# First expert step of a mixture-of-experts layer: token rows by zero-one products on TensorE in place of an indirect DMA

## Chip, cores and metric

One core of a Trainium2 chip. The metric is the device time of one execution in microseconds (us), lower is better. A moment such as 1291.30 is counted in us from the start of the profiled execution.

## What is computed

The program runs two transformer stacks on 256 tokens of width 1024. The change touches only the end of each of the second stack's two layers (`DEPTH = 2`, 272 tokens with the 16 meta tokens), its mixture of experts:

```
grp_prob = softmax(t @ w_grp + b_grp); g_prob, g_sel = top_k(grp_prob, 1)
in_grp = the 8 expert logits of the chosen group; e_prob, e_sel = top_k(softmax(in_grp), 2)
combine = one_hot(8 * g_sel + e_sel, 32) * gate, summed over the two
hid = silu(t @ w1[e]) * (t @ w3[e])
y = sum over e of (hid * combine) @ w2[e]
h = layer_norm(ALPHA * h + y)
```

There are 32 experts; `w1` and `w3` are 1024 x 256 each, `w2` is 256 x 1024, all float32. Every token goes to two of them.

## The kernel before

Tokens live mostly as `hT` (features on partitions). After the first layer norm of a layer they are also turned into rows, `h_tok` (tokens on partitions, three blocks of 128, 128 and 16, `TOK`), which lies in `h_area`. ScalarE writes those rows (six copies, each counted on the semaphore `htok_ready`), and SyncE stores them to HBM as `h_rows` (L944).

**Steps.** The experts are taken in 8 groups of 4. A step `s` serves one group: four experts side by side with 32 token slots each, 128 slots in all. A group in which an expert has more than 32 tokens takes further steps. The profiled input has 24 steps, 12 in each layer. VectorE computes the router's outcome: `comb` (gates), `rank` (the place of a token in its expert), and from them for a step a zero-one matrix `sel` (token x slot, 3 blocks; `select`, L2897 to 2905, counted on `sel_ready`). `sel` and `slot_cols` are single buffers. TensorE multiplies `sel` with `slot_cols` (`slots`, L1692 to 1697, PSUM bank `UP`) and gets for each slot its gate and its token number; VectorE copies these out (`slots_out`, L2907 to 2913). GpSimd turns the token number into an index and fetches the 128 rows from `h_rows` in HBM with an indirect DMA (`fetch`, L2242 to 2248, semaphore `rows_in`) into `x_rows`, which is the first block of `h_tok`. TensorE transposes the rows (`turn_rows`, L1699 to 1704, eight transposes into the banks `ROWS`), ScalarE copies them into `x_g` (L2189 to 2194), and the step proper starts (`expert_step`, L1716): 64 instructions of the up part (L1724), then the rows of the next step are turned, then the down part (L1746) and the sum into the output banks (L1757, L1759).

**First step of a layer.** `slots(start)`, then `hold_clock(..., 10)`: ten products of constants (L1177) whose result is overwritten, then the wait for the fetched rows, `turn_rows` twice, and `slots(start + 1)`. VectorE meanwhile computes how many steps each group needs (L2917 to 2950, `steps_ready`) and the selection of the second step (`select_at(start + 1)`).

**Expert weights.** A group's weights are 12 pieces of 1 MB, written (group, piece) below, each loaded by SyncE in one DMA (`expert_load`, all at L929) into one of 22 places. 22 pieces are loaded ahead of the loop, each as soon as its place is free. From (1, 10) on, a load waits in SyncE's program order for the step that gives its place free: pieces 0 to 7 of a group use the place of an earlier group's `w1`, `w3` and wait for the up part of that group's last step (`loop_full[UP]`, L961). Pieces (1, 4) and (1, 5) lie in `h_area` over the second and third blocks of `h_tok`; (1, 4) waits for the store to `h_rows` (`rows_out`).

Of the kernel before, what the change touches and what calls it, by code (L numbers as in the profile page):

```python
# [16 lines left out]
P = 128  # L17
# [99 lines left out]
def build(nc, A, out):  # L117

    ctx = ExitStack()
    with ctx:  # L120
# [750 lines left out]
        def _(sp):  # L871
# [37 lines left out]
            for slot, parts, last, *more in chunk_order:  # L909
# [10 lines left out]
                if slot == "experts":  # L920
# [24 lines left out]
                    sp.wait_ge(comb_ready, l + 1)  # L945
                    expert_load(1, 3)
                    expert_load(1, 9)
                    sp.wait_ge(rows_out, 48 * (l + 1))
                    expert_load(1, 4)
                    b, u = tiles[("rk", l)]  # L950
                    sp.wait_ge(full[b], u)
                    expert_load(1, 0)
                    for g in range(1, 8):
                        for m in range(10 if g == 1 else 0, 12):
                            g0, m0 = divmod(12 * g + m - XS, 12)
                            if m0 == 0:
                                if g0 == 0:
                                    sp.wait_ge(steps_ready, l + 1)

                                last = sp.value_load(steps[0:1, l, g0 + 10:g0 + 11], min_val=0, max_val=1000)  # L960
                                sp.wait_ge(loop_full[UP], up_use(last, l, 1))  # L961
                            elif m0 == 8:
                                end = sp.value_load(steps[0:1, l, g0 + 1:g0 + 2], min_val=1, max_val=1000)
                                sp.wait_ge(loop_full[ROWS[1]], row_use(end, l, 0))
                            expert_load(g, m)
# [21 lines left out]
        def _(pe):  # L987
# [186 lines left out]
            def hold_clock(b, count):  # L1174

                for _ in range(count):
                    nc.tensor.matmul(ps[:, b, 0:S1], ones[:, :], held, start=True, stop=True)  # L1177
# [197 lines left out]
            for l in range(DEPTH):  # L1375
# [311 lines left out]
                def begin_l(b, before):  # L1687

                    pe.wait_ge(loop_free[b], before + 1)
                    return b  # L1690
# [8 lines left out]
                def turn_rows(a, before):  # L1699
# [3 lines left out]
                        last = nc.tensor.transpose(ps[:, b, k * P:(k + 1) * P], x_rows[:, (4 * a + k) * P:(4 * a + k + 1) * P], ident)  # L1703
                    last.then_inc(loop_full[b], 1)

                pe.wait_ge(sel_ready, start + (2 * l + 1))
                slots(start, up_use(start, l, -2))
                hold_clock(begin_l(ROWS[0], row_use(start, l, -1)), 10)
                pe.wait_ge(rows_in, start * 16 + 16 * (l + 1))
                for a in range(2):  # L1710
                    turn_rows(a, row_use(start, l, -1))
                pe.wait_ge(sel_ready, start + (2 * l + 2))
                slots(start + 1, up_use(start, l, -1))
                pe.wait_ge(steps_ready, l + 1)
# [1 line left out]
                def expert_step(s, g):  # L1716
# [10 lines left out]
                                                    start=(k == 0), stop=(k == KT - 1))  # L1727
                    last.then_inc(loop_full[b], 1)

                    pe.wait_ge(rows_in, s * 16 + 16 * (l + 2))  # L1730
                    turn_rows(0, row_use(s, l, 0))
                    pe.wait_ge(ehid_ready, s + 1)
                    b = begin_l(UP, up_use(s, l, 1))
# [482 lines left out]
        def _(pool):  # L2216
# [7 lines left out]
            for l in range(DEPTH):  # L2224
                if l == 0:
                    pool.wait_ge(const2_in[0], 16 * 10)
                for lv in range(7):
                    for n in range(3):
                        if lv >= LV[n]:
                            continue  # L2230
                        L = TOK[n][1]
                        if lv == 0:
                            pool.wait_ge(lt_ready, 3 * l + n + 1)
                        else:
                            b, u = tiles[("X", l, lv - 1, n)]
                            pool.wait_ge(full[b], u)
                            if lv == 1:
                                pool.wait_ge(t_ready, t_at[l][(0, n)])
                        nc.gpsimd.tensor_tensor(heads(As[:, n, :])[0:L, :, 0:L], heads(LT[:, n, :])[0:L, :, 0:L],  # L2239
                                                levels[0:L, lv, 0:L].unsqueeze(1).broadcast_to([L, DH, L]), ALU.mult).then_inc(as_ready, 1)  # L2240

                def fetch(s):  # L2242

                    pool.wait_ge(slots_ready, s + (2 * l + 1))
                    nc.gpsimd.tensor_copy(row_of[:, :], slot_token[:, bass.ds(s, 1)])  # L2245
                    nc.gpsimd.drain()
                    nc.gpsimd.indirect_dma_start(x_rows, None, h_rows, bass.IndirectOffsetOnAxis(ap=row_of[:, :], axis=0))\
                        .then_inc(rows_in, 16)

                start = 0 if l == 0 else pool.value_load(steps[0:1, 0, 8:9], min_val=1, max_val=MAX_STEPS // 2)  # L2250
                pool.wait_ge(rows_out, 48 * (l + 1))
                fetch(start)
                pool.wait_ge(loop_full[ROWS[1]], row_use(start, l, 0))
                fetch(start + 1)
                pool.wait_ge(steps_ready, l + 1)
                last = pool.value_load(steps[0:1, l, 17:18], min_val=1, max_val=MAX_STEPS - 4)
                with nc.gpsimd.Fori(start, last) as s:
                    pool.wait_ge(loop_full[ROWS[1]], row_use(s, l, 1))
                    fetch(s + 2)
# [3 lines left out]
        def _(dve):  # L2263
# [303 lines left out]
            for l in range(DEPTH):  # L2567
# [386 lines left out]
                def select_at(s):  # L2954

                    g = dve.value_load(step_group[0:1, bass.ds(s, 1)], min_val=0, max_val=7)
                    select(g, pass_at[:, bass.ds(s, 1)])

                select_at(start + 1)
                slots_out(start + 1, up_use(start, l, 0))  # L2960
                stop = dve.value_load(steps[0:1, l, 8:9], min_val=1, max_val=MAX_STEPS - 3)
# [52 lines left out]
```

## Time and profile before

| | |
|---|---|
| time, median of 3 runs | 2179.34 us (2172.04 to 2183.63) |
| span of the profiled execution | 2178.0 us |
| the profiled execution's own time | given by its span alone; it lies 1.3 us under the median |
| TensorE busy | 92% of the span |
| VectorE, ScalarE, GpSimd busy | 43%, 34%, 32% |
| expert steps | 12 in layer 0 (from 1305.34), 12 in layer 1 (from 1905.94) |

A page of the profile gives busy time, granted TensorE clock ("PEclk") and DMA load by slices of the span, then the groups of instructions with what each waited for. The timeline of an engine lists its instructions in order: start, length, engine, line, operation, tiles, and in brackets how long the engine had been idle and what ended that. PE is TensorE, PEld its weight loads, DVE VectorE, ACT ScalarE, POOL GpSimd, SP SyncE; a letter q behind an engine is its sequencer. A float32 product shows as two records in the timeline, a transpose as one. The granted clock is 1.00 at 2.4 GHz and 0.50 at 1.2 GHz.

### The profile page before, as it was taken

The numbers are of one execution on the slowest core, as the hardware profiler recorded it, in microseconds if no ns is written. First come the engines' busy times: TensorE is split into PE (matmuls) and PEld (weight loads), VectorE is DVE, ScalarE is ACT, GpSimd is POOL, SyncE is SP. The second block draws the span as 40 slices with busy tenths as digits, with TensorE's granted clock in tenths as the row PEclk, the third lists the DMA queues.
The fourth block names the chain that finished last, engine by engine and source line by source line (L and its number), as shares of the span: only waits on it lengthen the run. The fifth ranks groups of instructions, "written<-read, shape, count | busy, mean of one in ns | idle before, by whom it ended". The sixth has DMA issues, their size and how long they took to land.

```text
span 2178.0 us, 36546 instructions
## 1 busy us (share of the span) xinstructions
PE 1999.3 (92%) x14251; PEld 1596.2 (73%) x14255; DVE 939.0 (43%) x1852; ACT 744.1 (34%) x1189; POOL 698.8 (32%) x558
## 2 busy tenths in 40 slices
PE   7989999999999999999999988759999999889966
PEld 6779899998889999987868763324578787634424
DVE  6562436615543456416754351111347643512212
ACT  5554543345555443413322222112223222222212
POOL 6557648885757558810003000000000030000000
PEclk9999999999999999999998989879999999999988
DMA  7335335553345345553310368999233203688693
GB/s 232 100 113 167 123 117 194 172 179 121 130 144 166 116 156 192 176 176 109 125 58 1 136 262 363 420 421 364 106 141 117 97 2 136 262 350 357 280 420 157
DMA packets 196269, 405.95 MB, mean 186 GB/s; under 512 B 18515, under 2 KB 143846, under 8 KB 171286
## 3 DMA queue, kind: packets, MB, share of 16 engines
q1 hardware_dynamic: 192374, 390.20, 48.8%
q0 software_dynamic: 3744, 13.63, 1.6%
q8 instruction: 107, 1.75, 0.3%
q14 instruction: 44, 0.36, 0.1%
HBM read 400.53 MB, written 3.28 MB: 185 GB/s over the span
## 4 chain that ended last, share of the span: by engine, by line
PE 71%; DVE 8%; DMA 7%; ACT 5%; SPq 3%; issue 2%; DVEq 2%; POOL 2%; ACTq 1%; POOLq 0%
PE ps L1017 9%; PE ps L1018 9%; PE ps L1356 9%; PE ps L1019 9%; PE ps L1724 7%; DMA weight_ring<-in_w 3%; PE ps L1746 3%; PE ps L1621 3%; SPq L929 3%; POOL weight_ring L2223 2%; DVEq L2266 1%; DMA last_pair<-in_w 1%; DMA spare<-in_w 1%; PE ps L1091 1%; PE ps L1560 1%
## 5 line engine op out<-in xcount | busy, mean ns | idle before, releaser
L2223 POOL TENSOR_TENSOR weight_ring<-weight_ring 128x512 fp32r<-128x512 f32 (+1 forms) x466 | 630.0, 1387 | 308.6 <-ACT weight_ring L1821 291.0
L1017 PE MATMUL ps<-weight_ring 128*128 128x256 f32 x1824 | 528.8, 290 | 12.4 <-DVE acts L2340 5.0
L1019 PE MATMUL ps<-weight_ring 128*128 128x256 f32 x1568 | 440.0, 281 | 0.0
L1018 PE MATMUL ps<-acts,weight_ring 128*128 128x256 f32 x1472 | 415.2, 282 | 0.0
L1017 PEld LDWEIGHTS ps<-weight_ring 128*128 128x128 f32 x1824 | 345.3, 189 | 25.5 <-issue 24.7
L1019 PEld LDWEIGHTS ps<-weight_ring 128*128 128x128 f32 x1568 | 298.4, 190 | 0.0
L1018 PEld LDWEIGHTS ps<-acts,weight_ring 128*128 128x128 f32 x1472 | 279.0, 190 | 1.9 <-issue 1.4
L1821 ACT ACTIVATE weight_ring<-weight_ring 128x2048 fp32r<-128x2048 f32 x128 | 238.7, 1883 | 92.0 <-PE ps L1019 82.8
L1356 PE MATMUL ps<-acts,weight_ring 128*128 128x272 f32 x896 | 212.8, 396 | 2.7 <-ACTq L2170 1.4
L2245 POOL CAST row_of<-slot_token 128x1 uint32 (+1 forms) x26 | 4.8, 186 | 625.1 <-DVE slot_token L2910 625.1
L1356 PEld LDWEIGHTS ps<-acts,weight_ring 128*128 128x128 f32 x896 | 170.3, 191 | 40.9 <-issue 2.4
L2239 POOL TENSOR_TENSOR acts<-work,tables 128x512 f32<-128x512 f32 (+1 forms) x36 | 38.4, 1090 | 465.2 <-DVE work L2710 398.7
L1724 PE MATMUL ps<-weight_ring,x_g 128*32 128x512 f32 x816 | 137.0, 654 | 32.3 <-DMA last_pair<-in_w 24.2
L1724 PE MATMUL ps<-acts,x_g 128*32 128x512 f32 x320 | 100.1, 628 | 26.6 <-DMA spare<-in_w 13.4
L2295 DVE TENSOR_TENSOR weight_ring<-weight_ring 128x512 fp32r<-128x512 f32 (+1 forms) x62 | 85.9, 1418 | 64.9 <-ACT weight_ring L1821 64.9
L2970 DVE SCALAR_TENSOR_TENSOR score<-score,slot_gate,ps 128x256 f32<-128x256 f32 x24 | 11.5, 481 | 237.5 <-ACT score L2199 237.5
L2199 ACT ACTIVATE score<-ps 128x256 f32<-128x256 f32 x24 | 9.2, 385 | 283.3 <-PE ps L1724 283.3
L1018 PE MATMUL ps<-qkv,weight_ring 128*128 128x256 f32 x352 | 99.6, 283 | 0.0
L1724 PEld LDWEIGHTS ps<-weight_ring,x_g 128*32 128x32 f32 x816 | 35.0, 119 | 87.8 <-issue 87.0
L1724 PE MATMUL ps<-spare,x_g 128*32 128x512 f32 x176 | 85.9, 646 | 0.0
L2978 DVE TENSOR_TENSOR z_gate<-ps,e_out 128x512 fp32r<-128x512 f32 x48 | 33.2, 692 | 118.2 <-ACT e_out L2205 118.2
L1724 PE MATMUL ps<-h_area,x_g 128*32 128x512 f32 x144 | 70.0, 643 | 14.1 <-DMA weight_ring<-in_w 14.1
(479 smaller groups left out, 3753.8 us busy)
## 6 DMA issues: line engine op xcount, KB each, us to landing
weight_ring<-in_w SPq DMA_DIRECT2D x112, 1024.0 KB, 22.8
weight_ring<-in_w_gate_up SPq DMA_DIRECT2D x44, 1024.0 KB, 5.0
weight_ring<-in_w_in SPq DMA_DIRECT2D x16, 2048.0 KB, 9.2
acts<-in_w SPq DMA_DIRECT2D x32, 1024.0 KB, 24.6
weight_ring<-in_x_wkv SPq DMA_DIRECT2D x16, 1024.0 KB, 5.3
weight_ring<-in_w_down SPq DMA_DIRECT2D x16, 1024.0 KB, 4.9
spare<-in_w SPq DMA_DIRECT2D x16, 1024.0 KB, 26.7
h_area<-in_w SPq DMA_DIRECT2D x16, 1024.0 KB, 23.5
```

The costliest lines, as they stand in the source:

```text
L929: sp.dma_start(expert_weights(g, m), src).then_inc(expert_in[pair_of(g, m)], 16)
L1017: nc.tensor.matmul(o, wh, xh, start=start, stop=False)
L1018: nc.tensor.matmul(o, wh, xr, start=False, stop=False)
L1019: return nc.tensor.matmul(o, wr, xh, start=False, stop=stop)
L1356: last = nc.tensor.matmul(ps[:, b, 0:S2], ring[:, slot, at + k * step:at + k * step + P], hT[:, k, :], start=(k == 0), stop=(k == KT - 1))
L1621: last = nc.tensor.matmul(ps[:, b, 0:S2], ring[:, s, at:at + P], oT[:, k, :], start=(k == 4), stop=(k == 3))
L1724: last = nc.tensor.matmul(ps[32 * j:32 * j + 32, b, :].rearrange("p (a n) -> p a n", a=2), x_g[:, k, 32 * j:32 * j + 32], expert_weights(g ...
L1746: last = nc.tensor.matmul(ps[32 * j:32 * j + 32, b, :], e_hidT[:, f, 32 * j:32 * j + 32], expert_weights(g, 8 + j)[:, at:at + 512], start= ...
L1821: nc.scalar.activation(r12(high[:, n % HIGH, 0:w]), raw[:, n % RAW, 0:w], ACT.Copy).then_inc(high_ready, 1)
L2223: nc.gpsimd.tensor_tensor(r12(w), w, r12(high[:, n % HIGH, part]).bitcast(F32), ALU.subtract).then_inc(rest_ready, 1)
L2239: nc.gpsimd.tensor_tensor(heads(As[:, n, :])[0:L, :, 0:L], heads(LT[:, n, :])[0:L, :, 0:L], levels[0:L, lv, 0:L].unsqueeze(1).broadcast_to ...
L2295: nc.vector.tensor_tensor(r12(w), w, r12(high[:, n % HIGH, 3 * k * 64:4 * k * 64]).bitcast(F32), ALU.subtract).then_inc(rest_ready4, 1)
```

## The change

The rows of the first step of each layer are no longer fetched. TensorE multiplies the token rows on chip with the selection: for each of 8 blocks of 128 features, three float32 products (one for each block of tokens, accumulated in PSUM), 24 in all, whose result is what the transposes gave before. They stand where the ten products of constants and the eight transposes stood. VectorE now makes the second step's selection only when these products are done, since they read `sel`; GpSimd's first fetch is that of the second step. The load of (1, 4), which overwrites rows that the products read, waits for them and goes behind (1, 0).

```
--- before
+++ after
@@ SyncE, behind the store of h_rows
                     expert_load(1, 3)
                     expert_load(1, 9)
-                    sp.wait_ge(rows_out, 48 * (l + 1))
-                    expert_load(1, 4)
                     b, u = tiles[("rk", l)]
                     sp.wait_ge(full[b], u)
                     expert_load(1, 0)
+                    start = 0 if l == 0 else sp.value_load(steps[0:1, 0, 8:9], min_val=1, max_val=MAX_STEPS // 2)
+                    sp.wait_ge(rows_out, 48 * (l + 1))
+                    sp.wait_ge(loop_full[ROWS[1]], row_use(start, l, 0))
+                    expert_load(1, 4)
@@ TensorE, first step
+                def gather_rows(a, before):
+
+                    b = begin_l(ROWS[a], before)
+                    for k in range(4):
+                        at = (4 * a + k) * P
+                        for n, (t0, L) in enumerate(TOK):
+                            last = nc.tensor.matmul(ps[:, b, k * P:(k + 1) * P], h_tok[0:L, n, at:at + P], sel[0:L, n, :],
+                                                    start=(n == 0), stop=(n == 2))
+                    last.then_inc(loop_full[b], 1)
+
+                pe.wait_ge(htok_ready, 6 * (l + 1))
                 pe.wait_ge(sel_ready, start + (2 * l + 1))
                 slots(start, up_use(start, l, -2))
-                hold_clock(begin_l(ROWS[0], row_use(start, l, -1)), 10)
-                pe.wait_ge(rows_in, start * 16 + 16 * (l + 1))
                 for a in range(2):
-                    turn_rows(a, row_use(start, l, -1))
+                    gather_rows(a, row_use(start, l, -1))
                 pe.wait_ge(sel_ready, start + (2 * l + 2))
                 slots(start + 1, up_use(start, l, -1))
...
-                    pe.wait_ge(rows_in, s * 16 + 16 * (l + 2))
+                    pe.wait_ge(rows_in, s * 16 + 16)
@@ GpSimd
                 pool.wait_ge(rows_out, 48 * (l + 1))
-                fetch(start)
                 pool.wait_ge(loop_full[ROWS[1]], row_use(start, l, 0))
                 fetch(start + 1)
@@ VectorE
+                dve.wait_ge(loop_full[ROWS[1]], row_use(start, l, 0))
                 select_at(start + 1)
```

TensorE in layer 0, from the first selection's products to the first up part, before and then changed (ISA and TENSOR_LOAD are its sequencer's; the loads read which steps the first group has):

```order
L1696 MATMUL ps<-slot_cols,sel 128x5 x3
L1177 MATMUL ps<-tables,ones 128x256 x10
L1703 MATMUL ps<-tables,h_area 128x128 x8
L1696 MATMUL ps<-slot_cols,sel 128x5 x3
L1770 TENSOR_LOAD steps
L1770 ISA x2
L1771 TENSOR_LOAD steps
```

```order
L1698 MATMUL ps<-slot_cols,sel 128x5 x3
L1714 MATMUL ps<-sel,h_area 128x128 x24
L1698 MATMUL ps<-slot_cols,sel 128x5 x3
L1781 TENSOR_LOAD steps
L1781 ISA x2
L1782 TENSOR_LOAD steps
```

Ten products of constants and eight transposes went, 24 products came; the sequencer's loads still stand behind the second selection's products.

VectorE at the same place, between the end of the step tables and the copy of the second step's token numbers, before and then changed:

```order
L2949 TENSOR_SCALAR pass_at<-pass_at 128x53
L2956 TENSOR_LOAD step_group [waits steps_ready]
L2956 ISA x2
L2899 ISA
L2899 COPY slot_cols<-comb 128x3x4
```

```order
L2959 TENSOR_SCALAR pass_at<-pass_at 128x53
L2966 TENSOR_LOAD step_group [waits loop_full2,steps_ready]
L2966 ISA x2
L2909 ISA
L2909 COPY slot_cols<-comb 128x3x4
```

The sequencer's load and all behind it now wait for `loop_full2`, the end of TensorE's new products.

SyncE behind the store of the rows, before and then changed (`acts`, `spare`, `h_area` and `last_pair` are the places of (1, 3), (1, 9), (1, 4) and (1, 0)):

```order
L944 DMA h_rows<-h_area 16x1024
L929 DMA acts<-in_w_2 128x2048 [waits comb_ready]
L929 DMA spare<-in_w_2 128x2048
L929 DMA h_area<-in_w_2 128x2048 [waits rows_out]
L929 DMA last_pair<-in_w_2 128x2048 [waits psum_full0]
L960 TENSOR_LOAD steps [waits steps_ready]
```

```order
L944 DMA h_rows<-h_area 16x1024
L929 DMA acts<-in_w_2 128x2048 [waits comb_ready]
L929 DMA spare<-in_w_2 128x2048
L929 DMA last_pair<-in_w_2 128x2048 [waits psum_full0]
L929 DMA h_area<-in_w_2 128x2048 [waits loop_full2,rows_out]
L962 TENSOR_LOAD steps [waits steps_ready]
```

(1, 4) went behind (1, 0) and behind TensorE's new products; nothing else on this queue moved.

## Rows read from the trace of the kernel before

**Rows 1.** The page: the span, and the DMA engines' busy share in 40 slices.

```profile
span 2178.0 us, 36546 instructions
...
DMA  7335335553345345553310368999233203688693
```

**Rows 2.** The chain of waits, layer 0: start, length, what.

```profile
1289.62 0.24 issue
...
1292.77 8.95 DMA h_area<-h_rows,row_of
```

**Rows 3.** TensorE's timeline, layer 0: start, length, instruction, idle before it.

```profile
1291.30 6.08 PE L1177 MATMUL ps<-tables,ones 128*128 128x256 f32 x20
1301.77 1.97 PE L1703 MATMUL ps<-tables,h_area 128*128 128x128 f32 x8 [4.38 <-DMA h_area<-h_rows,row_of]
1303.53 1.37 PE L1696 MATMUL ps<-slot_cols,sel 128*128 128x5 f32 x6
1305.34 8.38 PE L1724 MATMUL ps<-weight_ring,x_g 128*32 128x512 f32 x64 [0.44 <-DVEq L2912]
```

**Rows 4.** TensorE's timeline, layer 1.

```profile
1892.81 7.39 PE L1177 MATMUL ps<-tables,ones 128*128 128x256 f32 x20
1903.67 1.09 PE L1703 MATMUL ps<-tables,h_area 128*128 128x128 f32 x8 [3.47 <-DMA h_area<-h_rows,row_of]
1904.60 0.82 PE L1696 MATMUL ps<-slot_cols,sel 128*128 128x5 f32 x6
1905.94 8.45 PE L1724 MATMUL ps<-weight_ring,x_g 128*32 128x512 f32 x64 [0.52 <-DVEq L2912]
```

**Rows 5.** SyncE's timeline, layer 0: the loads of expert weights.

```profile
1289.54 0.33 SPq L929 DMA_DIRECT2D h_area<-in_w  x1
...
1313.79 0.33 SPq L929 DMA_DIRECT2D weight_ring<-in_w  x1
```

**Rows 6.** Busy time by stretch: engines, then granted clock, DMA share, GB/s.

```profile
1301.50:1313.80 12.30, 11.60 (x79) 5.34 (x80) 1.76 (x8) 2.49 (x4) 1.13 (x2) 0.73 0.13 44
1314.50:1344.40 29.90, 24.77 (x205) 12.96 (x206) 7.01 (x22) 8.34 (x13) 2.27 (x4) 1.00 1.00 406
```

**Rows 7.** GpSimd's fetches: issue of the second, landings of layers 0 and 1.

```profile
1306.26 0.95 POOL L2247 DMA_INDIRECT h_area<-h_rows,row_of  x1 [0.84 <-issue]
...
DMA to landing us min/median/max: 4.4/6.7/8.9
...
DMA to landing us min/median/max: 9.3/9.3/9.3
```

**Rows 8.** TensorE's timeline, float32 products of this shape elsewhere.

```profile
1166.45 1.06 PE L1570 MATMUL ps<-weight_ring,yT 128*128 128x128 f32 x8
1167.34 1.06 PE L1568 MATMUL ps<-yT,weight_ring 128*128 128x128 f32 x8
```

**Rows 9.** Busy time and granted clock by stretch, as rows 6.

```profile
1291.30:1294.38 3.08, 3.08 (x8) 2.52 (x8) 2.55 (x10) 0.00 (x0) 1.45 (x2) 0.50 1.00 423
...
1301.60:1308.02 6.42, 5.82 (x30) 3.77 (x34) 1.40 (x7) 2.48 (x3) 1.13 (x2) 0.50 0.01 4
...
1345.80:1349.00 3.20, 3.20 (x20) 0.92 (x16) 0.00 (x0) 0.00 (x0) 0.00 (x0) 0.50 1.02 419
...
1892.81:1898.54 5.73, 5.73 (x15) 4.56 (x15) 3.89 (x15) 0.00 (x0) 1.41 (x2) 0.50 1.01 420
...
1905.68:1908.39 2.71, 2.45 (x12) 0.61 (x16) 1.02 (x7) 1.28 (x1) 1.14 (x2) 0.50 0.00 0
```

**Rows 10.** VectorE's timeline, layer 0: the second step's selection.

```profile
1295.77 0.19 DVE L2949 TENSOR_SCALAR pass_at<-pass_at 128x53 f32<-128x53 f32 x1
1297.14 0.17 DVE L2899 COPY slot_cols<-comb 128x12 f32 x1 [1.18 <-issue]
1297.27 0.88 DVE L2901 SCALAR_TENSOR_TENSOR sel<-tables,pass_at,rank 128x128 f32<-128x128 f32 x3
```

**Rows 11.** TensorE's sequencer, layer 1: its load of the first group's steps.

```profile
L1770 PEldq TENSOR_LOAD <-steps x1: 305/305/305, 1903.9 to 1903.9; - x1
```

## The prediction

> **What bounds the kernel now.** I read the page first: over a span of 2178.0 us the DMA engines are nearly full in two stretches, slices 24 to 28 and again towards the end [rows 1], which are the expert loops of the two layers. Next the chain of waits around the entry of the first loop: from 1292.77 it is one piece of 8.95 us, the indirect fetch of the first step's rows [rows 2]. TensorE's timeline shows what that means: the ten products of constants end at 1297.38, TensorE idles 4.38 us for the fetch, turns the rows, multiplies the second selection and starts the first step at 1305.34 [rows 3]. Layer 1 has the same shape: 3.47 us idle, first step at 1905.94 [rows 4]. So the entry of the loop is bounded by the fetch, twice in the program, and 4.38 + 3.47 = 7.9 us is all the idle time there is to win directly.
>
> Does an earlier start reach the end? SyncE's next expert load is issued at 1313.79, as soon as the up part ends (1305.34 + 8.38 = 1313.72) [rows 3, 5]. Before it the DMA engines are nearly empty (share 0.13), behind it full (1.00) for at least 30 us [rows 6]. The loads behind it are released by steps. An earlier first step therefore moves the whole loop, its DMA-bound stretches too, and I count a gain at the first step at its full size.
>
> **What goes.** The fetch: 8.95 us in layer 0, 9.3 in layer 1, 4.4 for the second fetch of layer 0 [rows 2, 7]. The ten products of constants, 6.08 and 7.39 us, and the eight transposes, 1.97 and 1.09 us [rows 3, 4].
>
> **What comes on the path, step by step.**
> (a) The products. 24 float32 products are 48 records. Float32 products of this shape at full clock follow each other 1167.34 - 1166.45 = 0.89 us per 8 records, 0.111 us each [rows 8]. At half clock I take twice that, 0.223; the eight transposes of layer 0, 1303.53 - 1301.77 = 1.76 us, were at 0.22 each with a granted clock of 0.50 [rows 3, 9]. The products begin where those of constants began. In layer 0 the clock there is 0.50 until 1294.38: 3.08 us, 14 records; the other 34 take 3.8 us, end at 1298.2. In layer 1 it is 0.50 for 5.73 us after 1892.81: 26 records; the other 22 take 2.5 us, end at 1901.0 [rows 4, 9]. I assume that the new products raise the clock at the same moment as the old ones, since both keep TensorE busy without a gap.
> (b) A new wait. VectorE's selection of the second step was made while the fetch ran, done by 1298.15 [rows 10]; now its sequencer waits for (a). From the end of the tables, 1295.96, to its first copy it took 1.18 us, most of it the sequencer's load of the step's group, which now stands behind the wait: 1.1 us. The selection itself: 1298.15 - 1297.14 = 1.0. From its drain to TensorE's products 0.24 us, say 0.3 [rows 2, 10]. Sum 2.4 us, all on the path. Behind VectorE's wait stand only the second step's token numbers, then the loop.
> (c) The second selection's products, then the start of the step: 0.82 + 0.52 = 1.34 us at full clock [rows 4]. But TensorE's sequencer reads the group's steps behind them; before, it did so ahead, during the transposes: from 1903.9 to the step's start at 1905.94 are 2.0 us [rows 4, 11]. Now it can't begin before the selection is ready. Bounds 1.3 and 2.0; I take 2.0, since that row is the same sequence of instructions.
> So a first step starts 2.4 + 2.0 = 4.4 us after its products end. Layer 0: 1302.6 against 1305.34, 2.7 us won. Layer 1: 1905.4 against 1905.94, 0.5 us won.
> (d) The clock in the first step. Before, a stretch at 0.50 reached 2.7 us into the up part in both layers (1305.34 to 1308.02; 1905.68 to 1908.39) [rows 9]. Now TensorE idles about 2.4 us in (b), then does light work. A similar pause elsewhere was followed by 3.20 us at 0.50 (1345.80 to 1349.00) inside an up part [rows 9], so I expect about 3 us, 0.2 us worse in each layer.
> Sum: 2.7 + 0.5 - 0.4 = 2.8, about 3 us.
>
> **What is covered.** ScalarE's copies into `x_g` follow the products and are done during (b). The load of (1, 4) was issued at 1289.54 [rows 5]; it now goes at about 1298.3, 1 MB at 406 GB/s, 2.6 us, into a time in which DMA is nearly empty [rows 6], and its group's weights are wanted only behind the first step. Nothing waits behind it on SyncE's queue but the load at 1313.79. The second fetch, issued at 1306.26, landed 4.4 us later [rows 7], 3 us before it was wanted at 1313.72. It moves with the step and meets empty DMA engines again. If that cover went, each us would cost one. GpSimd does nothing else there.
>
> A rule that speaks against the change: by the Trainium skill (DMA: Bandwidth & Descriptors, Anatomy of one DMA) a GpSimd DMA takes about 2.0 us plus bytes / 436e3, for these 512 KB 3.2 us as an estimate. By that the rows would be in at 1296.0 and 1897.6, before the products of constants end; the old first steps would start 3.57 and 2.27 us behind that end, at 1301.0 and 1902.5, and the change would lose 1.6 + 2.9, about 5 us, to some 2184. The trace disagrees, 8.95 and 9.3 us behind queued weight loads [rows 2, 7]; only the fetch that met empty engines, 4.4 us, is near the rule.
>
> **The rivals.**
> *The clock is kind* (13%). Products wholly at full clock take 48 x 0.111 = 5.3 us, end 1296.6 and 1898.1, steps start at 1301.0 and 1902.5: 4.3 and 3.4 us won, and 1.3 us more per layer if no slow stretch (2.7 us at half) falls into the step. 10.3 us, 2169. For it: the slow stretch differs by layer, 3.08 against 5.73 us [rows 9]. Against: both layers were slow at this point.
> *The clock is unkind, and the new chain is the longer one* (17%, the side of slower). Products wholly at 0.50: 48 x 0.223 = 10.7 us, end 1302.0 and 1903.5, steps at 1306.4 and 1907.9, 1.1 and 2.0 us lost, 2182. It decides when more than about 38 (layer 0) or 30 (layer 1) of the 48 records run at 0.50. If the up part were at 0.50 throughout as well, another 5.7 us each (5.70 us were at full clock): 2194, 4% of the 17. For it: layer 1 has already 26 slow records, and 5-column products and pauses surround them. Against: unbroken work did bring the clock back in both layers.
> *The gain is swallowed by the weight loads* (10%), 2179. For it: the loop is DMA-bound behind the first step. Against: its first load is released by that step, with DMA at 0.13 before it [rows 6].
> That the change doesn't do what it says I leave out: the order of instructions shows 24 products for the fetch.
>
> The Trainium skill (TensorE: Matmul & The Clock Gate, What you observe and What's actually happening) says that the half rate is the default, that activity lifts it, and that the point of the switch varies from run to run. Rows 9 agree: 3.08 and 5.73 us for the same code.
>
> **How the numbers follow.** The forecast has 60%: 2179.3 - 3 = 2176.3; the span would be 2175. Runs before scattered by 11.6 us, a median of a few by perhaps 4 us either way. The range takes the kind rival at 2169 with a little scatter and the unkind one at 2182 with some: 2168 to 2184. A measurement of this kernel can tell about 0.5%, 11 us, from no change. Faster by more: half of the kind rival and 2 of the forecast's 60, 0.09. Slower by more: 0.05 from the unkind rival's far end and scatter. Else 0.86.
>
> **What would show it.** Right: no idle time before TensorE's rows; 48 records of `sel`, `h_area` in 6 to 9 us; then about 2.4 us idle until VectorE's selection; first steps 1 to 3 us earlier, counted from the first selection's products; (1, 4) issued behind the products; the load behind the up part earlier by the same. Wrong: products much longer than 9 us, an idle TensorE before the second step's rows or before group 1's weights, or loops that end at the old distance although they begin earlier. The forecast fails most simply if the clock's phase at the two entries is another one.

## The result, and the profile after the change

| | before | after |
|---|---|---|
| time, median | 2179.2 us (2172.0 to 2183.6, 4 runs) | 2192.4 us (2188.9 to 2194.7, 4 runs) |
| ratio, 95% interval | | 1.0058 [1.0041, 1.0074] |
| profiled execution: time, span | span 2178.0 | 2188.93, span 2187.1 |
| first selection's products to the first up part, layers 0 and 1 | 15.47, 14.58 us | 20.75, 20.59 us |

The change costs 13.2 us. The forecast was 2176.3 in a range of 2168 to 2184, with 5% on slower by over 0.5%. It was wrong in sign and the range missed the time by 8 us.

(Two corrections to the sections on the kernel before. Piece (1, 4) alone covers the second and third blocks of `h_tok`; (1, 5) lies behind it. And a span is 1.8 to 1.9 us shorter than the time of the same execution in every run listed, so the profiled execution of the kernel before took about 2179.8 us, close to the median and not 1.3 us under it.)

The page after, which answers to [rows 1]:

```profile
span 2187.1 us, 36622 instructions
...
DMA  7335335553444355553310369998334103688693
```

The two stretches of full DMA are where they were. The entries are counted from the first selection's products, and the first up parts to the transposes behind them. In the kernel before these lines, which no group of rows has, stand for both layers:

```profile
1289.87 1.50 PE L1696 MATMUL ps<-slot_cols,sel 128*128 128x5 f32 x6 [0.73 <-DVEq L2905]
1313.65 0.66 PE L1703 MATMUL ps<-tables,h_area 128*128 128x128 f32 x4
1891.36 1.52 PE L1696 MATMUL ps<-slot_cols,sel 128*128 128x5 f32 x6 [1.02 <-DVEq L2905]
1914.32 0.66 PE L1703 MATMUL ps<-tables,h_area 128*128 128x128 f32 x4
```

The place of the change is shown by TensorE's timeline, layer 0, which answers to [rows 3] (L1698 are the selection's products, L1714 the new ones, L1735 the up part, L1705 the next step's transposes):

```profile
1285.72 1.50 PE L1698 MATMUL ps<-slot_cols,sel 128*128 128x5 f32 x6 [0.36 <-DVEq L2915]
1287.15 15.06 PE L1714 MATMUL ps<-sel,h_area 128*128 128x128 f32 x48
1304.42 1.53 PE L1698 MATMUL ps<-slot_cols,sel 128*128 128x5 f32 x6 [2.21 <-DVEq L2915]
1306.47 8.90 PE L1735 MATMUL ps<-weight_ring,x_g 128*32 128x512 f32 x64 [0.52 <-DVEq L2922]
1315.30 0.66 PE L1705 MATMUL ps<-tables,h_area 128*128 128x128 f32 x4
```

The same in layer 1, which answers to [rows 4]:

```profile
1893.51 1.53 PE L1698 MATMUL ps<-slot_cols,sel 128*128 128x5 f32 x6 [1.06 <-DVEq L2915]
1894.96 15.06 PE L1714 MATMUL ps<-sel,h_area 128*128 128x128 f32 x48
1912.06 1.53 PE L1698 MATMUL ps<-slot_cols,sel 128*128 128x5 f32 x6 [2.04 <-DVEq L2915]
1914.10 8.87 PE L1735 MATMUL ps<-weight_ring,x_g 128*32 128x512 f32 x64 [0.52 <-DVEq L2922]
```

Read it against steps (a) to (c). No idle time stands ahead of the new products, but they take 15.06 us in both layers, 0.314 us a record, where (a) had 6.9 and 8.2 us in all. Behind them come the 2.21 and 2.04 us of VectorE's wait, the second selection and the up part. The stretches, as [rows 9]:

```profile
1285.70:1302.21 16.51, 16.49 (x54) 12.81 (x54) 4.64 (x19) 0.60 (x1) 0.00 (x0) 0.50 0.42 172
1302.21:1306.40 4.19, 1.53 (x6) 1.43 (x6) 1.30 (x7) 1.88 (x2) 0.08 (x1) 0.50 0.73 246
1306.40:1310.12 3.72, 3.65 (x20) 1.00 (x24) 1.46 (x6) 0.00 (x0) 1.23 (x2) 0.50 0.21 76
1893.50:1910.02 16.52, 16.51 (x54) 12.82 (x54) 4.81 (x20) 0.60 (x1) 0.00 (x0) 0.50 0.36 152
```

The granted clock is 0.50 over all of them. TensorE was busy for 16.49 of 16.51 us in the first stretch, and for 16.51 of 16.52 in layer 1, and its clock did not rise; it rose only at about 1310.12, 3.7 us into the up part. The weight loads of the products in layer 0, by form (busy, mean ns, and idle time before them with its cause):

```profile
L1714 PEld LDWEIGHTS ps<-sel,h_area 128*128 128x128 f32 x32 | 7.4, 322 | 1.6 <-issue 1.6
L1714 PEld LDWEIGHTS ps<-sel,h_area 16*128 16x128 f32 x16 | 4.0, 308 | 1.8 <-issue 1.8
```

Between the loads lie 1.6 + 1.8 us put down to "issue". 48 records at half clock are 10.7 us by the prediction, so 4.4 us of the 15.06 are not the clock's, and this column holds 3.4 of them.

The other engines did as forecast. VectorE, layer 0, as [rows 10]: its selection of the second step starts after 11.51 us without work, behind the wait for the products:

```profile
1303.34 0.17 DVE L2909 COPY slot_cols<-comb 128x12 f32 x1 [11.51 <-issue]
```

SyncE, as [rows 5]: (1, 4) goes as soon as the products end, and the first load of the loop 1315.44 - 1315.30 = 0.1 us after the up part:

```profile
1302.31 0.33 SPq L929 DMA_DIRECT2D h_area<-in_w  x1
1315.44 2.58 SPq L929 DMA_DIRECT2D weight_ring<-in_w  x5
```

GpSimd, as [rows 7]: the fetch of the second step's rows and its landing, 5.5 us, during the up part:

```profile
1307.38 1.13 POOL L2258 DMA_INDIRECT h_area<-h_rows,row_of  x1 [0.88 <-issue]
...
DMA to landing us min/median/max: 5.5/5.5/5.5
```

**Where the 13.2 us are.** I cut both profiled executions at the first selection's products, at the first up part and at the transposes behind it. The entries grew by 5.28 and 6.01 us, the first up parts (to their transposes) by 0.52 and 0.43: 12.2 us. The stretch between the layers grew by 0.50 and the rest behind layer 1's by 0.51: 13.3 us. The spans differ by 9.1 only, because this execution reached the first selection 4.15 us earlier (1285.72 against 1289.87), in code that the change doesn't touch. That 13.3 is also the difference of the medians is in part luck: after's profiled execution is the fastest of its four, 3.5 us under their median.

### The profile page after: what moved, and what is told of

Its sections match the earlier page's. It is cut to its first block, busy times and chain, and to the rows that moved or that the text cites. A ratio compares the mean times of both kernels' runs of the same rounds, so it can differ in the third digit from the quotient of the medians.

```text
span 2187.1 us, 36622 instructions
## 1 busy us (share of the span) xinstructions
PE 2014.3 (92%) x14291; PEld 1605.0 (73%) x14295; DVE 938.7 (43%) x1852; ACT 744.1 (34%) x1189; POOL 695.1 (32%) x554
## 4 chain that ended last, share of the span: by engine, by line
PE 72%; DVE 7%; DMA 6%; ACT 5%; SPq 3%; DVEq 2%; issue 2%; POOL 2%; ACTq 1%; POOLq 0%
PE ps L1019 9%; PE ps L1020 9%; PE ps L1021 9%; PE ps L1358 9%; PE ps L1735 7%; DMA weight_ring<-in_w 3%; PE ps L1757 3%; PE ps L1623 3%; SPq L929 3%; POOL weight_ring L2234 2%; DVEq L2276 1%; PE ps L1714 1%; DMA last_pair<-in_w 1%; DMA spare<-in_w 1%; PE ps L1093 1%
## 5 line engine op out<-in xcount | busy, mean ns | idle before, releaser
L1735 PE MATMUL ps<-weight_ring,x_g 128*32 128x512 f32 x816 | 139.4, 667 | 32.5 <-DMA last_pair<-in_w 24.2
L1735 PE MATMUL ps<-acts,x_g 128*32 128x512 f32 x320 | 100.2, 629 | 25.9 <-DMA spare<-in_w 12.5
L1735 PEld LDWEIGHTS ps<-weight_ring,x_g 128*32 128x32 f32 x816 | 34.9, 121 | 90.6 <-issue 90.4
L1735 PE MATMUL ps<-spare,x_g 128*32 128x512 f32 x176 | 86.0, 646 | 0.0
L1735 PE MATMUL ps<-h_area,x_g 128*32 128x512 f32 x144 | 70.2, 645 | 13.8 <-DMA weight_ring<-in_w 13.8
```

Source lines behind the costliest of these rows:

```text
L1735: last = nc.tensor.matmul(ps[32 * j:32 * j + 32, b, :].rearrange("p (a n) -> p a n", a=2), x_g[:, k, 32 * j:32 * j + 32], expert_weights(g ...
```

## The experiments

Four theories of the 15.06 us stood against each other. S: the third product of each block reads 16 rows and not 128. D: it is the zero-one data. W: one product of 128 columns for each of TensorE's weight loads is too light a work, whatever its rows. P: it is the phase of the clock at the entry, by chance. The table gives the cuts for each kernel's one profiled execution: the new products, the entry, the first up part to the next transposes (layer 0, layer 1), and the stretch between the layers. Ratios are to the kernel before, measured beside each (medians 2179.0 to 2179.5); the three kernels with a single run have none, and their times say little. e1b and e2b leave out part of the computation, as said there.

| kernel | median us (runs) | ratio | products | entry | up part | between |
|---|---|---|---|---|---|---|
| before | 2179.2 (4) | | none | 15.47, 14.58 | 8.31, 8.38 | 577.7 |
| after | 2192.4 (4) | 1.0058 | 15.06, 15.06 | 20.75, 20.59 | 8.83, 8.81 | 578.2 |
| e1b_repeat | 2181.5 (1) | | 7.14, 8.21 | 12.86, 13.59 | 9.68, 8.70 | 582.8 |
| e2b_constants | 2188.9 (1) | | 15.06, 15.06 | 20.75, 20.60 | 8.85, 8.78 | 578.3 |
| e3b_hold | 2194.0 (1) | | 8.41, 8.41 | 21.48, 20.96 | 8.50, 8.59 | 577.9 |
| e4b_grouped | 2189.8 (7) | 1.0041 | 10.61, 10.32 | 16.32, 15.87 | 9.40, 9.29 | 582.5 |
| e5_two | 2190.0 (5) | 1.0050 | 15.06, 15.06 | 18.38, 18.49 | 8.36, 9.70 | 578.0 |
| e6_padded | 2180.8 (10) | 1.0002 | 7.16, 8.23 | 12.86, 13.59 | 9.70, 8.70 | 582.8 |
| e7_padded_two | 2176.0 (11) | 0.9984 | 7.03, 8.32 | 10.72, 10.95 | 8.70, 7.00 | 582.0 |
| e8_no_constants | 2186.4 (10) | 1.0032 | none | 15.55, 14.27 | 9.79, 8.49 | 582.7 |
| e9_after_hold9 | 2196.4 (4) | 1.0086 | 15.06, 15.06 | 20.24, 20.59 | 9.12, 8.79 | 578.5 |
| e10_before_hold9 | 2179.4 (10) | 1.0006 | none | 15.40, 14.02 | 9.84, 8.63 | 582.7 |
| e11_padded_two_hold9 | 2173.7 (12) | 0.9969 | 7.25, 8.25 | 10.08, 10.88 | 7.01, 7.00 | 578.0 |

**The row count.** The second block in place of the short third one, so that the rows of the third block (16 tokens) are left out of the first step:

```
-                        for n, (t0, L) in enumerate(TOK):
-                            ... h_tok[0:L, n, at:at + P], sel[0:L, n, :], start=(n == 0), stop=(n == 2))
+                        for i, n in enumerate((0, 1, 1)):
+                            ... h_tok[:, n, at:at + P], sel[:, n, :], start=(i == 0), stop=(i == 2))
```

> The third product of each block of features (16 tokens, 16 rows of the array) is replaced by a second product with the second block of 128 tokens, so the rows of step one are wrong in value; 48 records as in the changed kernel, all with 128 rows. The changed kernel took 15.06 us for its 48 records in both layers, 0.314 each, granted clock 0.50 throughout. Theory S (the 16-row products break the overlap of weight loads and products, and leave the array so empty that the clock is not given back): 0.22 us a record at half clock, the clock comes back during the products, 6 to 10.7 us in all, first step some 5 to 9 us sooner in each layer. Theory D (the nearly all-zero selection is what leaves the clock down): 0.22 or 0.31 a record, clock 0.50 to the end, 10.7 to 15 us. Theory W (one 128-column float32 product per weight load is too light whatever its rows): 0.314 a record, 0.50, 15 us. Theory P (phase by chance): 0.314 at 0.50 and half that after a random moment.

TensorE's timeline, two stretches of the products and their weight loads, layer 0:

```profile
1289.29 7.14 PE L1714 MATMUL ps<-sel,h_area 128*128 128x128 f32 x48
...
1300.71 9.74 PE L1735 MATMUL ps<-weight_ring,x_g 128*32 128x512 f32 x64 [1.07 <-DVEq L2922]
...
1289.29:1292.70 3.41, 3.41 (x18) 3.41 (x18) 2.81 (x12) 0.00 (x0) 0.00 (x0) 0.53 0.98 408
1292.90:1296.40 3.50, 3.50 (x32) 3.33 (x30) 0.89 (x4) 0.60 (x1) 0.00 (x0) 1.00 0.60 250
...
L1714 PEld LDWEIGHTS ps<-sel,h_area 128*128 128x128 f32 x48 | 6.9, 236 | 0.0
```

As many records take 7.14 us. The clock comes back about 3.5 us into them, and no load waits (0.0, mean 236 ns over both clocks). In layer 1 they take 8.21 us; there the clock is at 0.51 over the first 5.6 us and at 1.00 after 1900.50. These are still products of 128 columns with a weight load each, so W falls, and what differs is the row count of every third product (and its data, which the next run settles). The loads of expert weights from HBM that run beside it are not the reason either: the DMA share is 0.98 here and was 0.42 in the slow kernel.

**The data.** The same shapes on constants, so that the first step gets no token rows at all:

```
-                            ... h_tok[0:L, n, at:at + P], sel[0:L, n, :],
+                            ... ones[0:L, :], ident[0:L, :],
```

> The products keep their shapes (128, 128 and 16 rows) and their number, but multiply ones by the identity, as the products of constants of the kernel before did; the rows of step one are wrong in value. Theory S: 15 us, 0.314 us a record, clock 0.50, as the changed kernel. Theory W: the same. Theory D: with the operands of the old constants the clock comes back, 8 to 12 us. Theory P: may come back at any moment.

```profile
1287.09 15.06 PE L1714 MATMUL ps<-tables,ones 128*128 128x128 f32 x48
...
1287.10:1302.10 15.00, 15.00 (x49) 11.39 (x48) 3.89 (x15) 0.60 (x1) 0.00 (x0) 0.50 0.38 156
```

The same 15.06 us at 0.50, so D falls. With e1b this leaves the row count.

**The clock at the start.** Ten products of constants ahead of the new ones, as they stood before the change:

```
+                hold_clock(begin_l(ROWS[0], row_use(start, l, -1)), 10)
                 for a in range(2):
                     gather_rows(a, row_use(start, l, -1))
```

> The ten products of constants are put back in front of the 24 products, nothing else. All theories: 6 to 8 us of constants, clock back at 1.00 during them. Then theories S, W and D: the 48 records at about half their time, 7 to 8 us, while the clock lasts, and it falls again within them or soon after; entry (first selection's products to first step) 1.5 + 7 + 8 + 4.3 = 20 to 22 us, no better than the changed kernel's 20.7. Theory P: clock stays up, 7.5 us, up part at full clock (7 us).

```profile
1292.39 7.56 PE L1179 MATMUL ps<-tables,ones 128*128 128x256 f32 x20
1299.79 8.41 PE L1714 MATMUL ps<-sel,h_area 128*128 128x128 f32 x48
...
1299.80:1308.20 8.40, 8.40 (x49) 6.40 (x47) 0.00 (x0) 0.60 (x1) 0.00 (x0) 1.00 0.00 0
```

A clock that had come back stayed at 1.00 through all 48 records, where theories S, W and D had let it fall within them or soon after; in layer 0 it fell in the pause behind them (the second selection's products take 1.53 us there), in layer 1 it held until they came (0.91 us). The 48 records took 8.41 us, 3.1 more than the 5.3 of 48 at 0.111 [rows 8]. Over the 16 times that the row count goes from 128 to 16 or back, that is about 0.19 us a change at full clock. At half clock it is (15.06 - 10.7) / 16 = 0.27 us.

**Fewer changes of the row count.** The loop over token blocks outside the one over features, so that the count changes 4 times and not 16:

```
+                    for n, (t0, L) in enumerate(TOK):
+                        for k in range(4):
...
+                                                    start=(n == 0 and k == 0), stop=(n == 2 and k == 3))
```

> Same 24 products, ordered by token block: four with the first block, four with the second, four with the 16 tokens, per bank; 4 changes of row count a layer in place of 16. Theory S: the changes cost (15.06 - 48 x 0.223) / 16 = 0.27 us each, so 12 fewer save 3.3 us a layer at half clock, 11.8 us for the products, and 2192 - 7 = 2185 us; if the clock also comes back, 8 to 10 us and 2181. Theories D, W: W says 15 us and 2192; D says 15 us or 10.7 at 0.50.

```profile
1291.80 10.61 PE L1714 MATMUL ps<-sel,h_area 128*128 128x128 f32 x48
...
1306.69 9.46 PE L1735 MATMUL ps<-weight_ring,x_g 128*32 128x512 f32 x64 [0.63 <-DVEq L2922]
...
1291.80:1301.00 9.20, 9.20 (x41) 8.74 (x40) 3.89 (x15) 0.60 (x1) 0.00 (x0) 0.50 0.62 257
1301.30:1304.50 3.20, 1.10 (x8) 0.91 (x8) 0.98 (x4) 1.05 (x2) 0.00 (x0) 1.00 0.33 41
1305.00:1311.00 6.00, 5.37 (x29) 2.02 (x33) 1.76 (x8) 0.33 (x1) 1.31 (x2) 0.50 0.54 197
```

10.61 us: the price of the changes is mostly gone. The 41 records of the first 9.20 us, short ones among them, follow each other at 0.224 us, the pace of 128-row products at half clock; so it is the change that costs, not the short product. But the clock comes back only at about 1301.3, some 9.4 us into the products, and stays for the pause behind them; the up part then begins in a new stretch at 0.50 and takes 9.46. So there are two costs: the changes of the row count, and a clock that stays low for longer than with products of 128 rows. The time is 1.0041 [1.0029, 1.0052], 2189.8 us and not the 2185 expected: the entries won 4.4 and 4.7 us against after's, but the up parts gave back 0.6 and 0.5, and in the profiled execution the stretch between the layers 4.3.

**VectorE's wait.** The first step's selection in a place of its own (a part of `z_gate` that is free there), so that VectorE need not wait for the new products:

```
+        sel1 = e_rest[:, 0:3 * P].rearrange("p (n c) -> p n c", n=3)
+        slot_cols1 = e_rest[:, 3 * P:3 * P + 24].rearrange("p (n c) -> p n c", n=3)
...
-                select(0, 0.0)
+                select(0, 0.0, sel1, slot_cols1)
...
-                dve.wait_ge(loop_full[ROWS[1]], row_use(start, l, 0))
                 select_at(start + 1)
```

> The changed kernel, but the first step's selection and its columns have buffers of their own, so that VectorE need not wait for the products to make the second selection. Entry (start of the first selection's products to the first up part) was 20.75 and 20.59 us in the changed kernel, 15.47 and 14.58 before. If VectorE's wait costs what the trace of the changed kernel shows, 2.2 and 2.0 us idle on TensorE go in each layer, entry 18.5 us, 2192.4 - 4.3 = 2188 us. Rival: the sequencer's loads of the group's steps or ScalarE's copies take the place of the wait, entry 20 us or more, 2191 us.

```profile
1292.67 15.06 PE L1716 MATMUL ps<-z_gate,h_area 128*128 128x128 f32 x48
...
1309.62 8.43 PE L1737 MATMUL ps<-weight_ring,x_g 128*32 128x512 f32 x64 [0.43 <-DVEq L2925]
```

The second selection's products follow without idle time, and the step starts 1309.62 - (1292.67 + 15.06) = 1.9 us behind the products, not 4.3. The entries are 2.4 and 2.1 us shorter, as expected. In layer 1 the up part gave 0.9 of it back. The time, 1.0050 [1.0030, 1.0070], can't be told from after's (1.0058 [1.0041, 1.0074]), so that these 4.5 us reach the end is not shown here.

**An earlier and longer hold of the clock.** In the kernel after, 9 products of constants and not 5 in the pause ahead of the routing:

```
-                hold_clock(begin("rk", l), 5)
+                hold_clock(begin("rk", l), 9)
```

> The changed kernel with 9 instead of 5 products of constants ahead of the ranks' products, which fill the 1.9 us that TensorE waits there for VectorE, so that the clock may still be at 1.00 when the selection's products begin. The question is whether it is the clock at the entry or the 16-row products that make them slow. If the clock at the entry (my forecast's view): products 8.4 us as in the run with constants in front, all at 1.00, entry 0.9 + 8.4 + 4.2 = 13.6 us, 2192.4 - 14 = 2178 us. If the 16-row products let the clock fall: they begin at 0.17 us a record and end at 0.31, 10 to 13 us in all, entry 15 to 18 us, 2182 to 2188 us. If the clock falls before them all the same (light products of 5 and 32 columns, the wait for the selection): 15 us, 2192.

```profile
1289.61 0.99 PE L1698 MATMUL ps<-slot_cols,sel 128*128 128x5 f32 x6 [1.45 <-DVEq L2915]
1290.54 15.06 PE L1714 MATMUL ps<-sel,h_area 128*128 128x128 f32 x48
...
1288.00:1290.00 2.00, 0.55 (x5) 0.42 (x4) 1.58 (x9) 0.00 (x0) 0.00 (x0) 1.00 0.99 277
1290.54:1305.60 15.06, 15.05 (x49) 11.38 (x48) 3.92 (x16) 0.60 (x1) 0.00 (x0) 0.50 0.41 169
```

The test of P. In layer 0 the clock was at 1.00 until the first selection's products (0.99 us against 1.50), fell between 1290.00 and 1290.54, and the new products took 15.06 us all the same. e11 below has the same work ahead of padded products, and its clock fell at the same place; they took 7.25 us. Over the eight entries of four kernels (after, e2b, e5, e9), at moments up to 5.6 us apart, the new products took 15.06 us each time, and 128-row ones never over 8.32. So P falls: it is what these products are, not when they come. Only behind 7 us of constants, in e3b, did the clock hold. What this run can't say is what they would take with the clock at 1.00 at their start and no constants ahead, since it fell before them. The time is 1.0086 [1.0064, 1.0108]; its interval overlaps that of after.

**Padded to 128 rows.** The third product over all 128 rows, the 112 unused ones of `h_tok` set to zero by ScalarE; here the whole computation is kept.

```
+                        nc.scalar.activation(h_tok[:, 2, :]..., ones[:, :]..., ACT.Copy, scale=0.0)
...
-                            ... h_tok[0:L, n, at:at + P], sel[0:L, n, :],
+                            ... h_tok[:, n, at:at + P], sel[:, n, :],
```

> The changed kernel with the third block's products over all 128 rows (16 token rows and 112 rows of zeros, which ScalarE writes in an idle moment); same result. Theory S (row count): products 7 to 8.2 us as with the repeated block, entry 13 to 14 us, up part 8.8 to 9.7; from first selection to end of up part 22.4 us against 23.8 and 23.0 before, about 1 us better a layer, 2177 us. Theory D or W, already weakened: 15 us, 2192.

```profile
1288.93 7.16 PE L1714 MATMUL ps<-sel,h_area 128*128 128x128 f32 x48
```

7.16 and 8.23 us: what step (a) had said of the change itself, 6.9 and 8.2. The time came back to before's, 1.0002 [0.9992, 1.0012], and no further.

**Padded, and without VectorE's wait** (e5 and e6 together).

> Both: third block over 128 rows, and own buffers for the first selection. If the two costs are separate, products 7 to 8.2 us and no idle time behind them, entry 1.5 + 7.7 + 0.9 + 0.5 = 10.6 to 12 us against 15.47 and 14.58 before, and some of the up part's slow stretch gone: 3 to 4 us a layer better than before, 2172 us. If the DMA-bound loop swallowed an earlier start: 2179.

```profile
1290.09 7.03 PE L1716 MATMUL ps<-z_gate,h_area 128*128 128x128 f32 x48
1297.30 0.92 PE L1700 MATMUL ps<-slot_cols,sel 128*128 128x5 f32 x6 [0.18 <-DVEq L2920]
```

Another 2.1 and 2.6 us off the entries, and 0.9984 [0.9974, 0.9995], 4.8 us under e6: here the copy of the buffer does reach the end.

**What the constants were worth.** The change also takes out ten products of constants. In the kernel before:

```
-                hold_clock(begin_l(ROWS[0], row_use(start, l, -1)), 10)
```

> The kernel before without the ten products of constants ahead of the fetched rows. If they only filled TensorE's wait for the fetch, nothing is lost but the clock: transposes and second selection at 0.50 (they were at 0.50 in layer 0, at 1.00 in layer 1), up part wholly or mostly at 0.50 at first: 8.4 to 10 us instead of 8.4, 0 to 2 us a layer, 2179 to 2183 us. If the time between first selection and step is the fetch's alone, entry stays at 15.5 and 14.6 to 15.5 us.

Timeline of TensorE, and from the chain of waits the fetch:

```profile
1290.27 1.50 PE L1696 MATMUL ps<-slot_cols,sel 128*128 128x5 f32 x6 [0.40 <-DVEq L2904]
1302.25 1.97 PE L1703 MATMUL ps<-tables,h_area 128*128 128x128 f32 x8 [10.48 <-DMA h_area<-h_rows,row_of]
...
1305.82 9.86 PE L1723 MATMUL ps<-weight_ring,x_g 128*32 128x512 f32 x64 [0.44 <-DVEq L2911]
...
1293.17 9.03 DMA h_area<-h_rows,row_of
```

The entry is as long as before (15.55, 14.27), since it is the fetch's, 9.03 us. But the time rose by 1.0032 [1.0019, 1.0044], 7 us: TensorE idles 10.48 us, and what follows is slower (layer 0's up part 9.86 against 8.38, layer 1's transposes 1.97 against 1.09). The mean granted clock of the whole program is 0.955 to 0.957 in nine of the ten runs, and 0.959 to 0.963 in those of the kernel before: it is a loss of clock. Where it lies is not shown: e10 below keeps the products, has before's time, and in its profiled execution the same long up parts (9.84, 8.63).

The fetch took 9.03 us with these products gone, at a DMA share of 0.88. The estimate by the Trainium skill (DMA: Bandwidth & Descriptors, Anatomy of one DMA), some 3.2 us, does not hold here behind queued loads.

**The longer hold (9 in place of 5, as in e9), in the kernel before and in e7.**

> The kernel before with the same 9 products of constants. Its entry ends with the fetch, so a faster clock ahead of it gives nothing there: entry 14.5 to 15.5 us, up part 7 to 8.5, 2177 to 2180 us. If the clock at the entry were worth more through what follows, 2172 to 2176.

> Third block over 128 rows, own buffers for the first selection, and 9 products of constants ahead of the ranks. If the clock stays at 1.00 through the entry: 0.9 + 5.4 for the products, then VectorE's selection (its tables are ready 6 us behind the first selection's products, so some 1 to 2 us of waiting), 0.9 + 1.2: entry 9 to 10 us against 10.7 and 11.0, up part 7.0 to 8.8: 2 to 3 us a layer better than without, 2171 us. If the clock falls as before: 2176.

In the kernel before it changes nothing, 1.0006 [0.9995, 1.0018]: there the fetch sets the entry. The padded kernel without VectorE's wait, layers 0 and 1:

```profile
1288.49 7.25 PE L1716 MATMUL ps<-z_gate,h_area 128*128 128x128 f32 x48
...
1297.75 7.07 PE L1737 MATMUL ps<-weight_ring,x_g 128*32 128x512 f32 x64 [1.13 <-DVEq L2927]
...
1893.62 7.07 PE L1737 MATMUL ps<-weight_ring,x_g 128*32 128x512 f32 x64 [0.52 <-DVEq L2927]
```

Both up parts are at 7.07 us, wholly at full clock. This execution is 6.2 us under the median of its kernel, so not every one need look like it. The time is 0.9969 [0.9954, 0.9983], 5.3 us under the kernel before: the lowest median of all and faster than both kernels, though by less than the 0.5% that I had called measurable. Its interval overlaps that of e7, so what the longer hold added is not shown.

**Left open: the stretch between the layers.** It takes 577.7 to 578.5 us in seven kernels and 582.0 to 582.8 in six, with the same code. In the kernel before, at one place between them (L1356, products of 272 columns behind light ones of 16):

```profile
1589.21 3.91 PE L1356 MATMUL ps<-acts,weight_ring 128*128 128x272 f32 x16
```

The same place in e8:

```profile
1592.45 6.75 PE L1356 MATMUL ps<-acts,weight_ring 128*128 128x272 f32 x16
```

16 records of L1356 take 6.75 us and not 3.91. The timelines of all thirteen kernels settle where the 4 to 5 us lie. From the transposes behind the first up part to the start of the light products ahead of this place it is 271.6 to 272.4 us in every one, so the first layer's loop keeps its length, whenever it begins. The group shown takes 3.91 us in the seven and 6.3 to 6.8 in the six, and by its end they are about 4 us behind. Whether it follows from how the clock left the entry, or falls by chance, one profile a kernel can't say. For chance speaks that the runs of the kernel before alone lie between 2172.0 and 2186.9 us. It may be why e6, whose entries with up parts are 1.9 us shorter than before's in all, has no better time, and why in e8's one execution this stretch is 5.0 us longer; e10's is as long, at the time of the kernel before. It may also be why the medians came out 2 to 5 us above what I had expected in e4b, e5, e6, e7, e8, e9 and e11, while the products and entries mostly met it. That too is open.

## Why the prediction was wrong

By its own steps:

- **(a) failed, and makes nearly all of the error of 16.1 us.** I priced the 24 products by rows of 128-row float32 products [rows 8] and by the sentence "I assume that the new products raise the clock at the same moment as the old ones, since both keep TensorE busy without a gap". Neither held for a third product of 16 rows. Measured against forecast: 15.06 - 6.9 = 8.2 us and 15.06 - 8.2 = 6.9, together 15.0; the forecast gain of 2.8 becomes a loss of 12.2, which is what the cuts show. The diff had `0:L`, and the order's fence printed the products under one shape, 128x128; I neither asked for the form of each product nor looked for a row on short ones.
- **Inside (a)** two things were missing. Of the 7.9 us in layer 0 between after's 15.06 and e6's 7.16, the changes of the row count are 15.06 - 10.7 = 4.4 and the clock that did not come back is the rest, 3.5; in layer 1 they are 4.4 and 2.5. A TensorE busy for 16.49 us of 16.51 did not raise the clock. Why it stays low beside 16-row products is open: the runs show that it does, not by what. The rule that I quoted from the Trainium skill (TensorE: Matmul & The Clock Gate, What's actually happening), that activity releases the half rate, is borne out by the padded products, 0.52 and then 1.00, and not by these, 0.50 over 15 us. The same page of the Trainium skill says that a load's time goes by its columns and that the row count doesn't matter (Step-by-step: what each phase is for). For one load the trace agrees, 322 against 308 ns; a sequence that mixes the counts pays 0.27 us a change all the same.
- **(b) and (c) held.** From the products' end to the step: 4.26 and 4.08 us, forecast 4.4. e5 took VectorE's part out and won 2.4 and 2.1 us, forecast 2.4. Of (c) both bounds came true: 2.05 and 2.04 us here, 1.87 in e6's layer 1 at full clock behind the wait, and 1.34 in layer 1 of e7 and e11, where TensorE did not wait for the selection.
- **(d) was somewhat too small:** 0.5 and 0.4 us in place of 0.2, since the clock was at 0.50 already and came back 3.7 us into the up part.
- **The cost of taking the constants out** was missing. I had counted them as something that goes, 6.08 and 7.39 us of filling. e8 puts their worth at 7 us (4 to 10). This is no further term of the 12.2: in the forecast the new products were to do the same work for the clock, and padded they did.
- **The cover held:** (1, 4), the second fetch (5.5 us, not waited for) and the weight loads behind the first step all moved with the step.

The rivals: the unkind clock had the right mechanism for 6.3 of the 15.0 us (3.8 and 2.5: 10.7 us at 0.50 in place of 6.9 and 8.2), and 17%. It could not give 15.06, since it knew no cost of changing the row count; its 2182 lies 10 us under the time. Its far end of 2194, with both up parts slow throughout, comes near only by accident. The kind clock did not occur. Swallowing by the weight loads did not either: the first loop kept its length within 0.8 us, though it began up to 5.4 us sooner after the first selection than in the kernel before (e11). The rival with a fetch of 3.2 us fell with the fetch's 8.95. My range ended where the unkind rival did, though I held the state of the clock for unknown and had no row for a 16-row product of this shape: that term should have been bounded from the slow side, and was not. The nearest row, the first selection's products (128, 128 and 16 rows, 5 columns, at 0.50), gives 1291.30 - 1289.87 = 1.43 us for 6 records, 0.24 each and 11.4 for 48. Even that would not have reached 15.06; that it could was not to be read from the trace before.

## What to carry to other kernels

Price a product by a row of its own form, row count included; a remainder block (here 16 of 128 rows) among full ones about doubled the time of all the products (15.06 us against 7.2 and 8.2), and padding it with zeros won back 11.6 us of the kernel. Ask of every TensorE instruction that goes what it did for the clock of the work behind it. A single buffer that a new reader keeps busy deserves a copy: 2.1 to 2.6 us for each entry here, 4.8 us of the kernel between e6 and e7.

## What the runs showed of the hardware that I had not expected

- With products over 16 rows between ones over 128 the granted clock stayed at 0.50 for 15 us of unbroken work (after, e2b, e5, e9); behind 7 us of constants it held at 1.00 (e3b). With the same count of records over 128 rows it came back after about 3.5 us in layer 0 and 5.7 in layer 1 (e1b, e6).
- A change of the row count between neighbouring products costs about 0.27 us at half clock and 0.19 at full (after, e3b). It does not depend on the data (e2b), and short products next to each other don't pay it: 41 records in 9.20 us at half clock (e4b).
- Ten products of constants in each layer's entry, whose result is thrown away, were worth 7 us of the kernel, though without them the entries were no longer: TensorE idled 10.48 and 9.09 us, and the program's mean granted clock fell from about 0.962 to 0.957 (e8).
